# A deeper software pipeline in the second attention of a two-block transformer kernel: all-row score passes, later transposes and value products, an earlier start of the output projection

## The chip, the cores and the metric

The kernel runs on one core of a Trainium2 chip. The metric is the device time of one execution in microseconds (us). Engines are named as in the profile: PE is TensorE's matmul side, PEld its weight loads, DVE VectorE, ACT ScalarE, POOL GpSimd, SP SyncE, which issues the DMAs.

## The reference, cut to what matters

Two transformer blocks are computed for 512 tokens of width 1024. The part that the change concerns is the last mixer of the second block, a sliding-window attention with 16 query heads of 64, which share 4 key and value heads (so 4 heads make a group g), and its output projection:

```python
q, z = split(h @ w_in); q = q * 64 ** -0.5
# 4 blocks of 128 queries; each sees its own 128 keys and the 128 before
logits = q @ k.T + alibi; logits = where(valid, logits, -inf)
m = maximum(max(logits), sink)
p = exp(logits - m); denom = sum(p) + exp(sink - m)
out = (p @ v) / denom
y = (out * silu(z)) @ w_out
h = h + rms_norm(y, b_post_g)
```

All matrices are float32. The kernel reaches that precision with pairs of rounded numbers: an operand is split into a high part and a rest, and a product is made of three passes (high by high, high by rest, rest by high).

## The kernel before, in words

**Order by hand.** `tensor_order()` writes TensorE's whole work as one list of blocks, ORDER, and BLOCK gives each its number. TensorE walks the list; before a block it waits until the PSUM bank of the block has been emptied (`BEFORE`, `emptied`) and until its inputs are there (`ready`). The other engines walk loops of their own and wait for block numbers (`pe_block`) and for semaphores of one another. All queues are in order.

**Weights.** SP loads each unit of weights in two halves into a ring of four buffers, `raw`. POOL splits a half in `split_half`: for the input projection (`q5`, `z5`) it first multiplies the rows with the norm's gain (L567), then it waits until the unit that last used the slot of `whi` and `wlo` has been multiplied (`last_block`), and makes the high part (L580) and the rest (L587). There are two slots, so a unit can be split while its neighbour is in use.

**The second attention.** It has 16 steps, a group g and a query block b each (`STEPS2`, b running fastest). Steps with b = 0 see 128 keys, the others 256, so they have one or two key tiles kt. They are pipelined over slots (`SLOTS2`). In slot i TensorE does, in this order:

- `o5` of step i - 2: the value product, three passes of 512 columns for each key tile, into bank 3,
- `t5` of step i - 1: four transposes of probabilities for each key tile, into bank 6 or 7,
- `s5` of step i: the scores. For each of the four heads a pass with the high part of the keys (L1644) and one with their rest (L1645), into banks 4 and 5,
- one or two half blocks ("Fk" and "F", 12 passes of 512 columns each) of the input projection for later groups (`PARTS2`; one in slots 4, 8 and 12). Finished blocks go to banks 0, 1 and 2 in turn.

The queries of a head lie in `q5` on 128 rows: 64 hold the high part and 64 the rest. The keys' high part lies twice, on rows 0 to 63 and 64 to 127, and so does the rest. L1644 therefore runs on all 128 rows; L1645 uses the 64 rows of the queries' high part alone.

**The other engines in slot i.** DVE: `scores2(i)` (bias of the group when b = 0, L1351; four additions of bias with maximum, L1360; L1364 and L1366), the rests of the transposed probabilities of step i - 1 (L1407), `probs2(i)` (L1372, L1374 and four multiplications, L1378), then the emptying of finished input-projection blocks (L1396 for `q5`, L1415 for the gate `z5`) and the products with the gate (`MEET2`, L1426, L1419). ACT: copies of finished blocks, the high parts of the transposes (L930), the copies of the value product (L935), the exponentials of step i (L944, L945), and L948. Probabilities lie in `tok`, two buffers.

**Output projection.** Block ("T", "f", c, kh, t) adds, for tokens t and output half c, the products with features 512 kh to 512 kh + 511, 12 passes. Its bank is t + 4c. Units come in the order (c, kh) = (0,0), (0,1), (1,0), (1,1). Blocks (0, 0, t) for t = 1, 2 stand at the end of slot 15 and t = 0 in slot 17; the other 13 follow the slots. The last steps are squares on ACT (L650), the root on POOL, two products on DVE for each half and token (L1432, L1443), and the store.

Of the kernel before, what the change touches and what calls it, by code (L numbers as in the profile page):

```python
# [7 lines left out]
P = 128  # L8
S = 512
T = S // P  # L10
D = 1024
KD = D // P
HALF = 512
# [5 lines left out]
NQ, NKV, DH = 16, 4, 64  # L19
# [10 lines left out]
def weight_units():  # L30
# [25 lines left out]
    u += [("f", 2 * c + kh, "T", "b_w_out_2", 4 * kh, 512 * c) for c in range(2) for kh in range(2)]  # L56
# [23 lines left out]
SLOTS2 = 18  # L80
# [3 lines left out]
MEET2 = {f: max(4 * (f // 2) + 6 + f % 2 * (f < 6), 2 + min(i for i in DONE2 if ("z5", f) in DONE2[i])) for f in range(8)}  # L84

# [8 lines left out]
def tensor_order():  # L94
# [45 lines left out]
    for i in range(SLOTS2):  # L140
        if i == 17:
            o += [("T", "f", 0, 0, 0)]
        if 2 <= i < 18:
            o += [("o5", i - 2)]
        if 1 <= i < 17:
            o += [("t5", i - 1, kt) for kt in ((0, 1) if STEPS2[i - 1][1] else (1,))]
        if i == 0:
            o += PARTS2[-1]
        if i < 16:
            o += [("s5", i, m) for m in range(2)]  # L150
        o += PARTS2.get(i, [])
        if i == 15:
            o += [("T", "f", 0, 0, t) for t in (1, 2)]
    o += [("T", "f", 0, 0, 3)] + [("T", "f", 0, 1, t) for t in range(T)]
    o += [("T", "f", 1, kh, t) for kh in range(2) for t in range(T)]
# [7 lines left out]
def bank_of(b):  # L163

    kind = b[0]
    if kind == "tr":
        name, t, j = b[1:]
        return {"x": (2 * t + j) % 4, "p": 4 + j, "x1": t + 4 * j, "h": (2 * t + j) % 4,
                "n": (2 * t + j) % 4}[name]
    if kind in ("F", "Fa", "Fk"):  # L170
        s, f = b[1:]
        if s in ("z4", "u4"):
            return 4 * (f // 2 % 2) + f % 2 + 2 * (s == "u4")
        if s == "k5":
            return 6 + f
        if s in ("q5", "z5"):
            return ([("q5", 0), ("q5", 1)] + JOBS2).index((s, f)) % 3
        return [x[1:] for x in ORDER if x[0] == "F"].index((s, f)) % 4
    if kind in ("T", "Th"):
        s, c, _, t = b[1:]  # L180
        return t + 4 * (1 if s == "v" else (c + (s == "v4")) % 2)
# [35 lines left out]
def program(nc, x, p, pre_norm_gain, w_in, lambda_q1, lambda_k1, lambda_q2, lambda_k2, subln_gain,  # L217
# [9 lines left out]
    with ctx:  # L227
# [40 lines left out]
        mhalf = sb("mhalf", [P, 1])  # L268
        ss_attn, ms_attn, r_attn = (sb(n, [P, NH1, T]) for n in ("ss_attn", "ms_attn", "r_attn"))
# [43 lines left out]
        prob2 = lambda s: tok[:, s % 2, :].rearrange("p (h k) -> p h k", h=4)  # L313
# [109 lines left out]
        def last_block(n):  # L423
# [8 lines left out]
            return BLOCK["T", s, j // 2, j % 2, T - 1]  # L432
# [206 lines left out]
        def _(act):  # L639
# [279 lines left out]
            for i in range(SLOTS2 + 2):  # L919
# [7 lines left out]
                for kt in ((0, 1) if STEPS2[i - 1][1] else (1,)) if 1 <= i < 17 else ():  # L927
                    b = ("t5", i - 1, kt)
                    act.wait_ge(pe_block, BLOCK[b])
                    A(pThi(kt), psum[bank_of(b)][:, :], ACT.Copy).then_inc(pt_hi[kt], 1)  # L930
                if 2 <= i < 18:
                    g, b = STEPS2[i - 2]
                    act.wait_ge(pe_block, BLOCK["o5", i - 2])
                    for m in range(2):
                        A(o5[m * DH:(m + 1) * DH, 2 * g:2 * g + 2, b * P:(b + 1) * P],  # L935
                          psum[3][0:DH, :].rearrange("p (f m s) -> p m f s", f=2, m=2)[:, m], ACT.Copy)\
                            .then_inc(o5_copied, 1)
# [11 lines left out]
            for c in range(2):  # L949
                for t in range(T):  # L950
                    act.wait_ge(pe_block, BLOCK["T", "f", c, 1, t])
                    square("f", t, c, psum[t + 4 * c][:, :])
# [3 lines left out]
        def _(dve):  # L956
# [388 lines left out]
            def scores2(i):  # L1345
# [8 lines left out]
                if i >= 2:  # L1354
                    dve.wait_ge(pe_block, BLOCK["t5", i - 2, 1])
# [46 lines left out]
            for i in range(SLOTS2 + 2):  # L1402
                if i < 16:
                    scores2(i)
                for kt in ((0, 1) if STEPS2[i - 1][1] else (1,)) if 1 <= i < 17 else ():
# [24 lines left out]
            def f_gain(c, t):  # L1430
                dve.wait_ge(squared["f"], T * c + t + 1)
                V.tensor_tensor(part_(t, c), psum[t + 4 * c][:, :], gain[:, 1, c * HALF:(c + 1) * HALF], ALU.mult)\  # L1432
# [15 lines left out]
        def _(pe):  # L1448
# [120 lines left out]
            def work(b):  # L1569
# [65 lines left out]
                if kind == "s5":  # L1635
# [4 lines left out]
                    rows = slice(m * DH, (m + 1) * DH)  # L1640
                    for j in range(2):
# [3 lines left out]
                        ins = M(out_, q[rows], klo(g)[rows, keys], start=False, stop=True)  # L1645
# [46 lines left out]
```

## Time and profile before

| | before |
|---|---|
| median of 3 runs | 993.23 us (992.97 to 993.75) |
| profiled execution, span from first to last instruction | 992.1 us |
| around the span (median less span) | 1.1 us |
| mean granted TensorE clock over the span | 0.982 |
| PE busy in the span | 940.2 us |
| DVE, ACT, POOL busy in the span | 450.7, 267.9, 638.9 us |
| first scores of the second attention start | 774.3 us |
| last matmul of the kernel starts | 986.04 us |

The profiled execution's own time stands as its span plus what lies around it; it is taken that the 1.1 us around it are the same for every version. The second attention and its output projection are the last 218 us of the span. A row of the timeline gives start, duration, engine, line, operation, operands and, in brackets, the idle time of the engine before it with what ended it. Durations of matmuls overlap, since they are pipelined: what a matmul costs is the distance between two starts.

### The profile page before, as it was taken

To read this page: it belongs to the slowest core of one execution; us is meant where nothing else is said; L and a number is where in the kernel's file an instruction comes from. 1 tells how busy PE (TensorE), PEld (TensorE's weight loads), DVE (VectorE), ACT (ScalarE), POOL (GpSimd) and SP (SyncE) were. 2 spreads that over 40 slices of the span, in tenths; PEclk is the share of its full clock that TensorE was granted. 3 is DMA by queue.
4 is the path that set the end of the run, shared out by engine and by line. 5 is a ranking of instruction groups with operands and counts; after the bars stand their busy time and mean duration, and the time that the engine had idled before them with its cause. 6 is when DMAs were issued, how large, how long until landed. Compare 5 with 4: busy or idle time off the path is not lost.

```text
span 992.1 us, 11937 instructions
## 1 busy us (share of the span) xinstructions
PE 940.2 (95%) x4304; PEld 758.5 (76%) x4304; DVE 450.7 (45%) x821; ACT 267.9 (27%) x679; POOL 638.9 (64%) x702
## 2 busy tenths in 40 slices
PE   4999999899999989999999999999979999898997
PEld 3787778678887768888888888888768777666776
DVE  4123445655144370004545204444678566857543
ACT  4123323321133241114111111110134335434421
POOL 7676455547789576768777766777776665633333
PEclk9999999999999999999999999999999899988999
DMA  7343121232422313232322233222311211102102
GB/s 204 121 126 96 56 85 42 70 123 86 142 74 91 100 64 128 90 101 85 106 86 86 94 99 100 91 86 85 107 64 64 65 53 54 57 29 64 42 3 85
DMA packets 71865, 84.30 MB, mean 85 GB/s; under 512 B 11264, under 2 KB 53760, under 8 KB 71808
## 3 DMA queue, kind: packets, MB, share of 16 engines
q1 hardware_dynamic: 71808, 83.54, 26.5%
q8 instruction: 35, 0.57, 0.2%
q14 instruction: 22, 0.18, 0.1%
HBM read 81.44 MB, written 2.10 MB: 84 GB/s over the span
## 4 chain that ended last, share of the span: by engine, by line
PE 78%; DVE 9%; POOL 5%; ACT 4%; issue 2%; DMA 1%; SPq 0%; POOLq 0%; DVEq 0%; ACTq 0%
PE bank L1454 23%; PE bank L1455 23%; PE bank L1456 23%; DVE tok L1378 2%; POOL wlo L587 2%; PE bank L1645 2%; ACT tok L944 2%; PE bank L1644 2%; PE bank L1621 1%; PE bank L1650 1%; PE bank L1585 1%; POOL ms L539 1%; POOL rstd L542 1%; ACT junk L650 1%; PE bank L1584 1%
## 5 line engine op out<-in xcount | busy, mean ns | idle before, releaser
L580 POOL TENSOR_SCALAR whi<-raw 128x512 fp32r<-128x512 f32 x280 | 185.8, 681 | 309.9 <-PE bank L1456 304.8
L587 POOL TENSOR_TENSOR wlo<-raw,whi 128x512 fp32r<-128x512 f32 x280 | 382.8, 1388 | 0.0
L1454 PE MATMUL bank<-actB_hi,whi 128*128 128x512 f32 (+1 forms) x416 | 163.2, 392 | 0.8 <-POOL wlo L587 0.8
L1455 PE MATMUL bank<-actB_lo,whi 128*128 128x512 f32 (+1 forms) x416 | 160.4, 385 | 0.0
L1456 PE MATMUL bank<-actB_hi,wlo 128*128 128x512 f32 (+1 forms) x416 | 160.3, 385 | 0.0
L1454 PE MATMUL bank<-whi,actA_hi 128*128 128x512 f32 x304 | 122.3, 402 | 9.9 <-DVE actA_lo L970 6.4
L1456 PE MATMUL bank<-whi,actA_lo 128*128 128x512 f32 x304 | 120.3, 396 | 0.0
L1455 PE MATMUL bank<-wlo,actA_hi 128*128 128x512 f32 x304 | 120.2, 395 | 0.0
L1454 PEld LDWEIGHTS bank<-actB_hi,whi 128*128 128x128 f32 x416 | 79.5, 191 | 17.8 <-DVE big L1265 0.9
L1456 PEld LDWEIGHTS bank<-actB_hi,wlo 128*128 128x128 f32 x416 | 79.2, 190 | 15.7
L1455 PEld LDWEIGHTS bank<-actB_lo,whi 128*128 128x128 f32 x416 | 79.6, 191 | 14.6
L1454 PE MATMUL bank<-actA_hi,whi 128*128 128x512 f32 x224 | 90.0, 402 | 0.0
L1455 PE MATMUL bank<-actA_lo,whi 128*128 128x512 f32 x224 | 87.9, 393 | 0.0
L1456 PE MATMUL bank<-actA_hi,wlo 128*128 128x512 f32 x224 | 87.7, 392 | 0.0
L1454 PEld LDWEIGHTS bank<-whi,actA_hi 128*128 128x128 f32 x304 | 57.7, 190 | 24.6 <-DVE actA_lo L970 7.8
L1454 PE MATMUL bank<-whi,actB_hi 128*128 128x512 f32 x192 | 75.1, 391 | 0.0
L1456 PE MATMUL bank<-whi,actB_lo 128*128 128x512 f32 x192 | 74.7, 389 | 0.0
L1455 PE MATMUL bank<-wlo,actB_hi 128*128 128x512 f32 x192 | 74.7, 389 | 0.0
L1456 PEld LDWEIGHTS bank<-whi,actA_lo 128*128 128x128 f32 x304 | 58.2, 191 | 12.4
L1455 PEld LDWEIGHTS bank<-wlo,actA_hi 128*128 128x128 f32 x304 | 58.1, 191 | 11.7 <-issue 0.2
L1454 PEld LDWEIGHTS bank<-actA_hi,whi 128*128 128x128 f32 x224 | 42.4, 189 | 10.8 <-issue 1.7
L1456 PEld LDWEIGHTS bank<-actA_hi,wlo 128*128 128x128 f32 x224 | 42.5, 190 | 9.0
(196 smaller groups left out, 1347.5 us busy)
## 6 DMA issues: line engine op xcount, KB each, us to landing
raw<-in_a_w_in SPq DMA_DIRECT2D x48, 512.0 KB, 3.6
raw<-in_w_in SPq DMA_DIRECT2D x32, 512.0 KB, 3.7
raw<-in_a_w_out SPq DMA_DIRECT2D x16, 512.0 KB, 3.3
raw<-in_b_w_in SPq DMA_DIRECT2D x16, 512.0 KB, 3.3
raw<-in_w_out SPq DMA_DIRECT2D x8, 512.0 KB, 3.8
raw<-in_w_ple_gate SPq DMA_DIRECT2D x8, 512.0 KB, 3.2
raw<-in_b_w_out SPq DMA_DIRECT2D x8, 512.0 KB, 3.4
resid<-in_x SPq DMA_DIRECT2D x4, 512.0 KB, 7.8
```

Source lines behind the costliest of these rows:

```text
L539: pool.tensor_scalar(m, ss[:, n, t, 0:1], ss[:, n, t, 1:2], EPS, ALU.add, ALU.add).then_inc(ms_ready[name], 1)
L542: pool.tensor_tensor(rstd[:, n, t:t + 1], m, mhalf[:, 0:1], ALU.pow).then_inc(rstd_ready[name], 1)
L580: pool.tensor_scalar(H, src[:, i * HALF:(i + 1) * HALF], 1.0, 1.0, ALU.mult, ALU.mult).then_inc(w_hi, 1)
L587: ins = pool.tensor_tensor(L, src[:, i * HALF:(i + 1) * HALF], H.bitcast(f32), ALU.subtract)
L650: A(junk[:, :], src, ACT.Square, scale=1.0 / 32, accum_out=ss[:, NORMS[name], t, c:c + 1])\
L944: A(pr, pr, ACT.Exp, bias=nmx[:, h:h + 1], accum_out=rs[:, h:h + 1]).then_inc(exp5, 1)
L1378: V.tensor_scalar(pr, pr, rr[:, h:h + 1], None, ALU.mult).then_inc(prob5, 1)
L1454: M(out_, whi_, xhi_, start=start, stop=False)
L1455: M(out_, whi_, xlo_, start=False, stop=False)
L1456: return M(out_, wlo_, xhi_, start=False, stop=stop)
L1644: M(out_, q, khi(g)[:, keys], start=True, stop=False)
L1645: ins = M(out_, q[rows], klo(g)[rows, keys], start=False, stop=True)
```

## The change

The value product moves from two slots behind the scores to three, the transposes from one to two. On DVE the loop body now does the probabilities of step i - 1 first, then the rests of step i - 2's transposes, then the scores of step i; ACT has the value copies and the transposes first, then finished blocks, then the exponentials. A third probability buffer, `prob3`, is added; to make room the reserve for dynamic DMA descriptors is set to 1024. The second score pass uses all 128 rows, so that the product of the two rests is added as well. Units of the output projection come in the order (0,0), (1,0), (0,1), (1,1), and all eight blocks with kh = 0 run in slots 15 to 18, in other banks.

```diff
-    u += [("f", 2 * c + kh, "T", "b_w_out_2", 4 * kh, 512 * c) for c in range(2) for kh in range(2)]
+    u += [("f", 2 * c + kh, "T", "b_w_out_2", 4 * kh, 512 * c) for kh in range(2) for c in range(2)]
...
-SLOTS2 = 18
+SLOTS2 = 19
...
-MEET2 = {f: max(4 * (f // 2) + 6 + f % 2 * (f < 6), 2 + min(i for i in DONE2 if ("z5", f) in DONE2[i])) for f in range(8)}
+MEET2 = {f: max(4 * (f // 2) + (7 + f % 2 if f < 6 else 6), 2 + min(i for i in DONE2 if ("z5", f) in DONE2[i])) for f in range(8)}
+FIRST_F = {15: ((0, 0), (0, 1)), 16: ((0, 2), (0, 3)), 17: ((1, 0),), 18: ((1, 2), (1, 3), (1, 1))}
+BANKS_F = ((0, 1, 2, 4), (5, 3, 6, 7))
...
     for i in range(SLOTS2):
-        if i == 17:
-            o += [("T", "f", 0, 0, 0)]
-        if 2 <= i < 18:
-            o += [("o5", i - 2)]
-        if 1 <= i < 17:
-            o += [("t5", i - 1, kt) for kt in ((0, 1) if STEPS2[i - 1][1] else (1,))]
+        if 3 <= i:
+            o += [("o5", i - 3)]
+        if 2 <= i < 18:
+            o += [("t5", i - 2, kt) for kt in ((0, 1) if STEPS2[i - 2][1] else (1,))]
...
-        if i == 15:
-            o += [("T", "f", 0, 0, t) for t in (1, 2)]
-    o += [("T", "f", 0, 0, 3)] + [("T", "f", 0, 1, t) for t in range(T)]
-    o += [("T", "f", 1, kh, t) for kh in range(2) for t in range(T)]
+        o += [("T", "f", c, 0, t) for c, t in FIRST_F.get(i, ())]
+    o += [("T", "f", c, 1, t) for c in range(2) for t in range(T)]
...
-        prob2 = lambda s: tok[:, s % 2, :].rearrange("p (h k) -> p h k", h=4)
+        prob2 = lambda s: (tok[:, 0, :], tok[:, 1, :], prob3[:, :])[s % 3].rearrange("p (h k) -> p h k", h=4)
...
-            for i in range(SLOTS2 + 2):
+            for i in range(SLOTS2 + 1):
+                if 1 <= i < 17:
+                    probs2(i - 1)
+                for kt in ((0, 1) if STEPS2[i - 2][1] else (1,)) if 2 <= i < 18 else ():
+                    dve.wait_ge(pt_hi[kt], i - 1 if kt else kt0_steps(i - 2))
+                    V.tensor_tensor(pTlo(kt), psum[bank_of(("t5", i - 2, kt))][:, :], pThi(kt).bitcast(f32),
+                                    ALU.subtract).then_inc(pt_lo[kt], 1)
                 if i < 16:
                     scores2(i)
-                for kt in ((0, 1) if STEPS2[i - 1][1] else (1,)) if 1 <= i < 17 else ():
-                    dve.wait_ge(pt_hi[kt], i if kt else kt0_steps(i - 1))
-                    V.tensor_tensor(pTlo(kt), psum[bank_of(("t5", i - 1, kt))][:, :], pThi(kt).bitcast(f32),
-                                    ALU.subtract).then_inc(pt_lo[kt], 1)
-                if i < 16:
-                    probs2(i)
...
                         M(out_, q, khi(g)[:, keys], start=True, stop=False)
-                        ins = M(out_, q[rows], klo(g)[rows, keys], start=False, stop=True)
+                        ins = M(out_, q, klo(g)[:, keys], start=False, stop=True)
...
-    nc = bacc.Bacc("TRN2", target_bir_lowering=False, num_devices=1)
+    nc = bacc.Bacc("TRN2", target_bir_lowering=False, num_devices=1, dynamic_dma_scratch_size=1024)
```

## Rows read from the trace of the kernel before

**Rows 1.** Waits of PE, 770 us to the end: waiter, releaser, us, times, longest.

```profile
PE bank L1650 <- DVE tok L1378: 10.2, 8, 3.6
```

**Rows 2.** PE's timeline in slots 1 and 2 of the attention.

```profile
783.76 0.63 PE L1650 MATMUL bank<-ident,tok 128*128 128x128 f32 x4 [1.80 <-DVE tok L1378]
...
785.06 0.55 PE L1645 MATMUL bank<-rests,parts 64*128 64x256 f32 x1
...
791.59 0.57 PE L1454 MATMUL bank<-actB_hi,whi 128*128 128x512 f32 x1
...
795.90 1.03 PE L1650 MATMUL bank<-ident,tok 128*128 128x128 f32 x8
796.69 0.36 PE L1644 MATMUL bank<-parts 128*128 128x256 f32 x1
...
799.17 0.50 PE L1454 MATMUL bank<-actB_hi,whi 128*128 128x512 f32 x1
```

**Rows 3.** The rest-of-keys pass, line 1645: ns min/median/max, first and last start.

```profile
L1645 PE MATMUL bank<-rests,parts x64: 322/381/580, 774.5 to 936.2; 64*128 64x256 f32 x48, 64*128 64x128 f32 x16
```

**Rows 4.** PE's timeline in the value projection: 256 columns, all rows, 21 steps between.

```profile
736.45 0.28 PE L1456 MATMUL bank<-v5hi,actB_lo 128*128 128x256 f32 x1
...
738.94 0.28 PE L1456 MATMUL bank<-v5hi,actB_lo 128*128 128x256 f32 x1
```

**Rows 5.** PE's timeline in the last 12 output blocks, 143 steps between.

```profile
953.53 0.47 PE L1454 MATMUL bank<-whi,actA_hi 128*128 128x512 f32 x1
...
986.04 0.39 PE L1456 MATMUL bank<-whi,actA_lo 128*128 128x512 f32 x1
```

**Rows 6.** Windows of 5 us: length, busy by engine, granted clock, DMA.

```profile
785.00:790.00 5.00, 5.00 (x12) 3.33 (x12) 2.73 (x11) 0.99 (x5) 0.00 (x0) 0.51 0.01 3
```

**Rows 7.** DVE's timeline: scores in slot 11, bias and scores in slot 12.

```profile
891.93 0.48 DVE L1360 CUSTOM_DVE_ANT_0 tok<-bank,smA,sinks 128x256 f32<-128x256 f32 x1
...
893.90 1.01 DVE L1364 TENSOR_SCALAR nmx<-mx 128x4 f32<-128x4 f32 x1
...
901.90 0.90 DVE L1351 TENSOR_SCALAR smB<-smC 128x256 f32<-128x256 f32 x4
...
904.03 0.17 DVE L1364 TENSOR_SCALAR nmx<-mx 128x4 f32<-128x4 f32 x1
```

**Rows 8.** DVE's timeline in slot 14, from the maxima to the probabilities.

```profile
927.33 0.17 DVE L1364 TENSOR_SCALAR nmx<-mx 128x4 f32<-128x4 f32 x1
...
927.61 1.28 DVE L1407 TENSOR_TENSOR pT<-bank,pT 128x512 fp32r<-128x512 f32 x2
929.93 0.16 DVE L1372 TENSOR_TENSOR den<-rs,esk 128x4 f32<-128x4 f32 x1 [1.04 <-ACT esk L945]
...
930.35 1.14 DVE L1378 TENSOR_SCALAR tok<-tok,rr 128x256 f32<-128x256 f32 x4
```

**Rows 9.** DVE's timeline in slot 3: the same four multiplications.

```profile
813.50 3.57 DVE L1378 TENSOR_SCALAR tok<-tok,rr 128x256 f32<-128x256 f32 x4
```

**Rows 10.** POOL's timeline: rests made in slot 3, and one unit split in slots 6 and 7.

```profile
813.80 2.63 POOL L587 TENSOR_TENSOR wlo<-raw,whi 128x512 fp32r<-128x512 f32 x2
...
834.45 1.20 POOL L580 TENSOR_SCALAR whi<-raw 128x512 fp32r<-128x512 f32 x2 [10.24 <-PE bank L1456]
...
841.21 2.55 POOL L587 TENSOR_TENSOR wlo<-raw,whi 128x512 fp32r<-128x512 f32 x2
```

**Rows 11.** Groups of instructions by form, 790 us to the end (busy us, mean ns).

```profile
L1378 DVE TENSOR_SCALAR tok<-tok,rr 128x256 f32<-128x256 f32 x48 | 20.0, 480 | 0.4
...
L1378 DVE TENSOR_SCALAR tok<-tok,rr 128x128 f32<-128x128 f32 x12 | 7.6, 698 | 0.1
...
L1366 DVE TENSOR_TENSOR den<-sinks,nmx 128x4 f32<-128x4 f32 x14 | 5.9, 421 | 0.5
L1364 DVE TENSOR_SCALAR nmx<-mx 128x4 f32<-128x4 f32 x14 | 5.7, 410 | 0.5
```

**Rows 12.** DVE's timeline: the last gate block, z5 of feature tile 7, emptied.

```profile
943.62 0.68 DVE L1415 SCALAR_TENSOR_TENSOR zg<-th,bank 128x512 f32<-128x512 f32 x1
```

More of the change, by code:

```diff
@@ L180, in bank_of @@
         s, c, _, t = b[1:]
+        if s == "f":
+            return BANKS_F[c][t]
         return t + 4 * (1 if s == "v" else (c + (s == "v4")) % 2)
@@ L268, in program @@
         mhalf = sb("mhalf", [P, 1])
+        prob3 = sb("prob3", [P, D])
         ss_attn, ms_attn, r_attn = (sb(n, [P, NH1, T]) for n in ("ss_attn", "ms_attn", "r_attn"))
@@ L431, in last_block @@
                 return BLOCK["F", s, 2 * j + 1]
-            return BLOCK["T", s, j // 2, j % 2, T - 1]
+            return max(BLOCK["T", s, j // 2, j % 2, t] for t in range(T))
         block = ctx.enter_context(nc.Block())
@@ L918, in _ @@
                 q5_out(f)
-            for i in range(SLOTS2 + 2):
+            for i in range(SLOTS2 + 1):
+                if 3 <= i < 19:
+                    g, b = STEPS2[i - 3]
+                    act.wait_ge(pe_block, BLOCK["o5", i - 3])
+                    for m in range(2):
+                        A(o5[m * DH:(m + 1) * DH, 2 * g:2 * g + 2, b * P:(b + 1) * P],
+                          psum[3][0:DH, :].rearrange("p (f m s) -> p m f s", f=2, m=2)[:, m], ACT.Copy)\
+                            .then_inc(o5_copied, 1)
+                for kt in ((0, 1) if STEPS2[i - 2][1] else (1,)) if 2 <= i < 18 else ():
+                    b = ("t5", i - 2, kt)
+                    act.wait_ge(pe_block, BLOCK[b])
+                    A(pThi(kt), psum[bank_of(b)][:, :], ACT.Copy).then_inc(pt_hi[kt], 1)
                 for s, f in DONE2.get(i - 1, ()):
@@ L926, in _ @@
                         A(th[:, :], psum[bank_of(("F", s, f))][:, :], ACT.Tanh, scale=0.5).then_inc(z5_tanh, 1)
-                for kt in ((0, 1) if STEPS2[i - 1][1] else (1,)) if 1 <= i < 17 else ():
-                    b = ("t5", i - 1, kt)
-                    act.wait_ge(pe_block, BLOCK[b])
-                    A(pThi(kt), psum[bank_of(b)][:, :], ACT.Copy).then_inc(pt_hi[kt], 1)
-                if 2 <= i < 18:
[L932 to L937, printed above, removed]
                 if i < 16:
@@ L950, in _ @@
                 for t in range(T):
-                    act.wait_ge(pe_block, BLOCK["T", "f", c, 1, t])
-                    square("f", t, c, psum[t + 4 * c][:, :])
+                    b = ("T", "f", c, 1, t)
+                    act.wait_ge(pe_block, BLOCK[b])
+                    square("f", t, c, psum[bank_of(b)][:, :])
         @block.vector
@@ L1353, in scores2 @@
                     dve.wait_ge(bias2_made, 4 * g + 4)
-                if i >= 2:
-                    dve.wait_ge(pe_block, BLOCK["t5", i - 2, 1])
+                if i >= 3:
+                    dve.wait_ge(pe_block, BLOCK["t5", i - 3, 1])
                 for h in (0, 2, 1, 3):
@@ L1401, in _ @@
             dve.wait_ge(dist_made, 4)
-            for i in range(SLOTS2 + 2):
+            for i in range(SLOTS2 + 1):
+                if 1 <= i < 17:
+                    probs2(i - 1)
+                for kt in ((0, 1) if STEPS2[i - 2][1] else (1,)) if 2 <= i < 18 else ():
+                    dve.wait_ge(pt_hi[kt], i - 1 if kt else kt0_steps(i - 2))
+                    V.tensor_tensor(pTlo(kt), psum[bank_of(("t5", i - 2, kt))][:, :], pThi(kt).bitcast(f32),
+                                    ALU.subtract).then_inc(pt_lo[kt], 1)
                 if i < 16:
                     scores2(i)
-                for kt in ((0, 1) if STEPS2[i - 1][1] else (1,)) if 1 <= i < 17 else ():
-                    dve.wait_ge(pt_hi[kt], i if kt else kt0_steps(i - 1))
-                    V.tensor_tensor(pTlo(kt), psum[bank_of(("t5", i - 1, kt))][:, :], pThi(kt).bitcast(f32),
-                                    ALU.subtract).then_inc(pt_lo[kt], 1)
-                if i < 16:
-                    probs2(i)
                 for f in (f for s, f in DONE2.get(i - 1, ()) if s == "q5"):
@@ L1431, in f_gain @@
                 dve.wait_ge(squared["f"], T * c + t + 1)
-                V.tensor_tensor(part_(t, c), psum[t + 4 * c][:, :], gain[:, 1, c * HALF:(c + 1) * HALF], ALU.mult)\
+                V.tensor_tensor(part_(t, c), psum[bank_of(("T", "f", c, 1, t))][:, :],
+                                gain[:, 1, c * HALF:(c + 1) * HALF], ALU.mult)\
                     .then_inc(f_gained, 1)
@@ L1639, in work @@
                     keys = slice((blk - 1) * P + k0, (blk + 1) * P)
-                    rows = slice(m * DH, (m + 1) * DH)
                     for j in range(2):
```

## The prediction

> **What bounds the kernel now.** I read the waits of PE first, then its timeline, then the queues that it waits for. PE is nearly always at work, but three things make the second attention long. The first is waits: eight times PE stood before a transpose until DVE had multiplied the probabilities, 10.2 us in all [rows 1]. The second is the clock. After the 1.80 us gap the matmuls of slot 1 soon stand twice as far apart, from about 785.1 to 791.9 us [rows 2], and the granted clock in that window is 0.51, the lower of the two levels, 1.2 GHz [rows 6]. Half of these 6.8 us is lost, 3.4 us. In the timeline the same follows the two other gaps of over 1.5 us in this stage, so 10.2 us in all. The third is the score passes themselves: in slot 2 eight of them take 799.17 - 796.69 = 2.48 us, 0.31 us each, though they have only 256 columns [rows 2]. Elsewhere passes of 256 columns on all 128 rows, each with a new weight load, start every 2.49 / 21 = 0.119 us [rows 4]. In the scores 128-row and 64-row passes alternate. The row speaks for that alternation as the price, not the columns. From the first to the last score pass of the stage there are 161.7 us [rows 3], about 10.7 us a slot.
>
> **All-row passes.** No row shows this alternation on all rows; the nearest is the value projection [rows 4], the same in columns, rows and alternating loads. I take 0.119 us, so 16 x 8 x 0.119 = 15.2 us instead of 16 x 8 x 0.31 = 39.7 us. Bounds: 0.31 (nothing won) and 0.10, what a transpose of 128 columns costs (0.79 us for eight, [rows 2]). The added arithmetic, rest by rest, has no instruction of its own.
>
> A page speaks against this part: the Trainium skill, "TensorE: Matmul & The Clock Gate", Part 3, says that a weight load overlaps a running matmul only where their row groups differ. By that rule two all-row passes overlap no better than before and the term stays 39.7 us; by the row it is 15.2 us. The value projection has equal row groups throughout and does not bear the rule out [rows 4].
>
> **PE's sum, if it never waited.** A 512-column pass costs 32.51 / 143 = 0.2273 us [rows 5], so a half block or an output block of 12 passes 2.73 us and a key tile of the value product 0.68 us. Four transposes cost 0.40 us [rows 2]. From the first score (774.3 us) to the end of the last score block (slot 15) PE now does 27 half blocks, 73.7 us; all scores, 15.2; value products of steps 0 to 12, 22 key tiles, 15.0; transposes of steps 0 to 13, 24 key tiles, 9.5. That is 113.4 us, up to 887.7 us. After it come 16 output blocks, 43.7 us, three value products, 4.1, and two steps of transposes, 1.6: 49.4 us.
>
> **The new loop over DVE and ACT.** With the deeper pipeline, probabilities are needed two slots later, so the old wait [rows 1] goes. What is late next is the loop that no depth shortens: DVE scores step i, ACT takes the exponentials, DVE multiplies, makes the rests of the transposes and only then scores step i + 1. From rows: scores to maxima 893.90 - 891.93 = 1.97 us [rows 7]; maxima to the first probability instruction, with the exponentials between, 929.93 - 927.33 = 2.60 us; two small instructions 0.42 us, four multiplications 1.14 us, two rests 1.28 us [rows 8]. Together 7.41 us. Bias and scores of a b = 0 step take 2.13 us in place of 1.97 [rows 7], and one slot in four has only one rest (0.64 us less), so 7.3 us on average. Other DVE work of a slot (emptied blocks, gate products) fits under the exponentials.
>
> To this comes what POOL does to DVE. The four multiplications took 1.14 us in slot 14 but 3.57 us in slot 3 [rows 8, 9], where POOL made two rests for 2.63 us [rows 10]. Against 0.285 us for a multiplication and 0.17 us for a small instruction [rows 8], the groups hold 20.0 - 13.7, 7.6 - 3.4, 5.7 - 2.4 and 5.9 - 2.4 us too much [rows 11], 17.3 us in some 15 slots, 1.2 a slot. No row shows how these meetings fall in the new order. Bounds: 0, and 1.9 if shorter slots bring more of them. I take 0.8, two thirds of the measured mean, because PE's full slots (two half blocks, scores, two key tiles: about 8.6 us) hide part of a stall. So 8.1 us a slot.
>
> On this the Trainium skill, "SBUF — State Buffer", section "SBUF: two separate sides", says that the port pair shared by the two engines is held for one whole instruction, so the loser would wait for one. By that, a stall would be half of what these rows suggest, the loop 7.7 us a slot, and the time that of rival (a). The trace shows a stall of 2.43 us, longer than either of the two POOL instructions [rows 9, 10].
>
> **Where PE and DVE meet.** In the new list the first output block (c = 0, t = 0) has bank 0, and the last block in it is z5 of tile 7, finished at the end of slot 14. DVE empties it (L1415) only after scores2(15). In the kernel before this gate came at 943.62 us [rows 12], and blocks t = 1 and 2, in other banks, stood in its place. So PE stops after the last scores for DVE's scores (1.97 + 0.29), the gate (0.6) and handovers (0.2), 3.1 us and the rests before them, and whatever DVE lags behind is paid here. A gap of 1.80 us was followed by the low clock [rows 2]; I add one such fall, 3.4 us (bounds 0 and 6.8).
>
> DVE's scores of step 2 start at the earliest when PE reaches them: 774.3 + three score blocks (2.9) + four half blocks (10.9) + one tile of transposes (0.4) = 788.5 us. With 13 slots of 8.1 us scores2(15) starts at 893.8, PE goes on at 896.9. Adding 49.4 and 3.4 gives 949.7 us for the last matmul; from there to the end of the span it was 992.1 - 986.4 = 5.7 us and nothing there changes. Span 955.4 us, and with the 1.1 us around it 956.5 us.
>
> **Edits that cost nothing.** Output weights: a slot is free after slot 16 and again after slot 18. Splitting an unscaled unit takes the 9.3 us of a scaled one [rows 10] less 1.84 us of scaling, 7.5 us; slots 17 and 18 give the first 14 us of cover, and the four blocks (0,1,t) give the second 10.9 us. Without that cover each would cost its 7.5 us. SP issues the same loads, in the changed order, and POOL the same splits. The last value copy and gate products come at the end of slot 18 under three output blocks, 8.2 us. The third buffer takes no instruction. The smaller descriptor reserve concerns no queue that the page lists for data; I price it at 0, with no row against it.
>
> **The rivals.** (a) PE bounds the stage: the meetings with POOL hide in PE's full slots. Then scores2(15) starts 0.6 us after the last scores, at 888.3, PE goes on at 891.4 and the time is 951.0 us with the fall of the clock, 947.6 without it. For it: PE's 113.4 us over 16 slots are 7.1 us a slot and full slots are longer than the bare loop. Against it: slots 4, 8 and 12 have one half block and the loop has no slack there. (b) POOL's stalls keep their mean or grow. At 1.2 us a slot scores2(15) starts at 899.0 and the time is 961.7 us; at 1.9, 970.8. For it: POOL's work is squeezed into less time. Against it: much of it may fall where DVE waits for PE. (c) All-row passes win nothing. PE's sum is 24.5 us more, DVE's loop hides, and the time is 975.5 us. Against it: rows 4. (d) Slower: each slot makes PE wait at its head for DVE (bank 4 scored, rests made), and each wait brings the clock down. A fall costs 3.4 us and at least the 1.8 us before it [rows 2], 5.2 us. From 947.6 us it takes more than nine falls to pass 993.2; ten give 999.6 us. For it: a gap of that size did this three times. Against it: a slot at half clock makes PE late, so that the next one has no gap, and two half blocks (5.5 us) stand between a slot's scores and the next slot's head.
>
> **How the numbers follow.** I give the forecast 0.55, (a) 0.22, (b) 0.16, (c) 0.04 and (d) 0.03. The range runs from 946, below (a) without a fall, to 971, the upper end of (b); (c) and (d) lie outside it, and some of the rest. About 0.2% (2 us) is what a measurement here can tell from no change. Slower comes from (d), 0.03; the same only from a mixture of (c) and (d), 0.01; the rest is faster.
>
> **What would show it.** Right: eight score passes in about 0.95 us; no wait of a transpose for L1378; one PE gap of 3 us or more before the first output block, ended by L1415, and a granted clock near 0.5 behind it; about 120 us from the first to the last score pass. Wrong: score passes still 0.31 us apart; gaps in front of every slot with low clock; waits of PE for POOL's L587 in the output projection; or no gap before the first output block.

## The result and the profile after

| | before | after |
|---|---|---|
| median | 993.49 us (four runs, 992.97 to 996.85) | 971.51 us (four runs, 967.63 to 974.51) |
| ratio | 1 | 0.9753, 95% interval 0.9722 to 0.9783 |
| profiled execution | span 992.1 us | 969.13 us, span 967.4 us |
| first maxima (L1364, after L1368) to the end of the span | 214.2 us | 190.6 us |
| us a slot, slots 2 to 15, by those maxima | 10.57 | 8.85 |

The kernel is faster by 22.0 us by the medians and by 24.7 us by the spans of the profiled executions; 36.7 us were forecast. The median lies 0.5 us above the upper end of the range, 971; the ratio times the 993.23 us that the forecast started from gives 968.7 us, which lies inside. Two measures are used below, "stage" (the row "first maxima to the end") and "us a slot", because they leave out what varies ahead of the stage: the first maxima come anywhere from 776.7 to 784.0 us in the ten profiled executions of the variants, which differ little there in code.

The page of the kernel after, engines and clock:

```profile
PE 909.9 (94%) x4304; PEld 747.7 (77%) x4304; DVE 456.6 (47%) x821; ACT 268.8 (28%) x679; POOL 638.1 (66%) x702
...
PEclk9999999999999999999999999999999999999899
```

PE has 30 us less busy time than the 940.2 us before. Most of it is the score passes: with them alone put back (E1) the page has 935.9 us.

PE's timeline of the kernel after (start, us, engine, line, operands; idle time before and what ended it in brackets): the eight score passes of slot 1, the two longest gaps, the last matmul.

```profile
779.53 0.28 PE L1648 MATMUL bank<-parts 128*128 128x256 f32 x1
...
780.48 0.40 PE L1459 MATMUL bank<-actB_hi,whi 128*128 128x512 f32 x1
...
810.50 0.42 PE L1459 MATMUL bank<-pT,parts 128*64 128x512 f32 x1 [3.64 <-DVE pT L1411]
...
904.00 0.28 PE L1649 MATMUL bank<-rests,parts 128*128 128x256 f32 x1
...
910.31 0.80 PE L1459 MATMUL bank<-whi,actA_hi 128*128 128x512 f32 x1 [6.04 <-DVE zg L1419]
...
913.47 0.50 PE L1460 MATMUL bank<-wlo,actA_hi 128*128 128x512 f32 x1
...
961.34 0.39 PE L1461 MATMUL bank<-whi,actA_lo 128*128 128x512 f32 x1
```

Eight passes now take 780.48 - 779.53 = 0.95 us, 0.119 us each, against 2.48 us in [rows 2] (1.03 us in the slots where they follow transposes). The wait of transposes for the multiplications [rows 1] has no row left. In its place stand these, from the waits of PE, 770 us to the end (waiter, releaser, us, times, longest):

```profile
PE bank L1459 <- DVE pT L1411: 8.3, 5, 3.6
...
PE bank L1459 <- DVE zg L1419: 6.0, 1, 6.0
...
PE bank L1648 <- DVE mx L1364: 2.1, 2, 1.4
```

The value product now waits for the rests that DVE makes of the transposed probabilities (L1411), and once PE waits 6.0 us for the gate (L1419). Who sets the pace is clearer from DVE's side. Groups of DVE in the stage of the kernel after, 776 to 915 us (busy us, mean ns; idle time before them):

```profile
L1382 DVE TENSOR_SCALAR tok<-tok,rr 128x256 f32<-128x256 f32 x32 | 16.9, 589 | 0.3
L1411 DVE TENSOR_TENSOR pT<-bank,pT 128x512 fp32r<-128x512 f32 x24 | 15.6, 683 | 2.2 <-ACT pT L933 2.0
L1382 DVE TENSOR_SCALAR prob<-prob,rr 128x256 f32<-128x256 f32 x16 | 9.5, 657 | 0.1
...
L1370 DVE TENSOR_TENSOR den<-sinks,nmx 128x4 f32<-128x4 f32 x16 | 7.0, 436 | 0.5
L1364 DVE CUSTOM_DVE_ANT_0 tok<-bank,smA,sinks 128x256 f32<-128x256 f32 x16 | 6.8, 478 | 0.0
...
L1376 DVE TENSOR_TENSOR den<-rs,esk 128x4 f32<-128x4 f32 x16 | 6.2, 387 | 15.2 <-ACT esk L948 15.1
...
L1368 DVE TENSOR_SCALAR nmx<-mx 128x4 f32<-128x4 f32 x16 | 4.8, 298 | 0.6
...
L1355 DVE TENSOR_SCALAR smB<-smC 128x256 f32<-128x256 f32 x8 | 3.7, 520 | 0.0
L1355 DVE TENSOR_SCALAR smA<-smC 128x256 f32<-128x256 f32 x4 | 3.4, 918 | 0.0
L1382 DVE TENSOR_SCALAR tok<-tok,rr 128x128 f32<-128x128 f32 x12 | 3.4, 348 | 0.1
...
L1382 DVE TENSOR_SCALAR prob<-prob,rr 128x128 f32<-128x128 f32 x4 | 0.9, 283 | 0.0
```

The scores (L1364) never stood idle for PE (0.0), and the rests waited for PE's transposes, through ACT's copies, for 2.0 us in the whole stage. Nearly all the rest of DVE's idle time is the exponentials inside the loop (L1376 for ACT, 15.1 us). So DVE and ACT set the pace and PE waits for them. The same groups in the kernel before, 777 to 942 us, three of them:

```profile
L1360 DVE CUSTOM_DVE_ANT_0 tok<-bank,smA,sinks 128x256 f32<-128x256 f32 x24 | 10.7, 482 | 16.0 <-PE bank L1645 15.8
...
L1372 DVE TENSOR_TENSOR den<-rs,esk 128x4 f32<-128x4 f32 x15 | 4.3, 288 | 18.3 <-ACT esk L945 18.3
...
L1351 DVE TENSOR_SCALAR smB<-smC 128x256 f32<-128x256 f32 x8 | 2.1, 326 | 0.0
```

There the scores still waited for PE: 16.0 us in this group alone.

The chain of waits of the kernel after, slots 13 to 15 (start, us, what), shows the loop without a stall and with one:

```profile
893.12 0.18 DVE nmx L1368
...
896.14 0.92 DVE tok L1382 x4
...
897.19 0.68 DVE pT L1411
...
899.53 0.18 DVE nmx L1368
...
902.80 1.65 DVE prob L1382 x2
...
904.49 1.97 DVE prob L1382 x2
906.46 1.19 DVE pT L1411 x2
...
909.29 0.18 DVE nmx L1368
...
909.58 0.69 DVE zg L1419
...
910.31 0.80 PE bank L1459
```

No piece of PE lies between 893.12 and 910.31. Slot 13 to 14 takes 6.41 us; slot 14 to 15 takes 9.76 us, because the four multiplications begin at 902.80 and end at 906.46, 3.66 us in place of 1.14. POOL's timeline in the same kernel:

```profile
903.09 2.60 POOL L590 TENSOR_TENSOR wlo<-raw,whi 128x512 fp32r<-128x512 f32 x2
```

Two rests by POOL, from 903.09 to 905.69, cover the stall. One by one, the multiplications take 0.48, 1.37, 1.35 and 0.70 us: the second and the third each end with one of the two rests, the last with the high part (L583) that POOL makes next. So an instruction of DVE loses to one instruction of POOL at a time. It is so all over the stage: of the kinds L1355, L1368, L1370, L1376 and L1382, 38 instructions take over 0.15 us more than their bare time, all 38 end at most 0.2 us behind the end of an instruction of POOL, and none loses more than that instruction took. This is the pair [rows 9, 10] again, now on the path that sets the end.

### The profile page after: what moved, and what is told of

It reads as the page before. It is cut to its first block, busy times and chain, and to the rows that moved or that the text cites. A ratio compares the mean times of both kernels' runs of the same rounds, so it can differ in the third digit from the quotient of the medians.

```text
span 967.4 us, 11936 instructions
## 1 busy us (share of the span) xinstructions
PE 909.9 (94%) x4304; PEld 747.7 (77%) x4304; DVE 456.6 (47%) x821; ACT 268.8 (28%) x679; POOL 638.1 (66%) x702
## 4 chain that ended last, share of the span: by engine, by line
PE 72%; DVE 14%; POOL 5%; ACT 5%; issue 3%; DMA 1%; SPq 0%; POOLq 0%; DVEq 0%; ACTq 0%
PE bank L1459 22%; PE bank L1460 22%; PE bank L1461 22%; POOL wlo L590 2%; ACT tok L947 2%; DVE tok L1382 2%; DVE tok L1364 2%; DVE pT L1411 1%; PE bank L1626 1%; PE bank L1590 1%; POOL ms L542 1%; POOL rstd L545 1%; ACT junk L653 1%; PE bank L1589 1%; PE bank L1599 1%
## 5 line engine op out<-in xcount | busy, mean ns | idle before, releaser
L583 POOL TENSOR_SCALAR whi<-raw 128x512 fp32r<-128x512 f32 x280 | 184.8, 678 | 286.1 <-PE bank L1461 280.8
L1459 PE MATMUL bank<-actB_hi,whi 128*128 128x512 f32 (+1 forms) x416 | 159.8, 384 | 0.8 <-POOL wlo L590 0.8
L1461 PEld LDWEIGHTS bank<-actB_hi,wlo 128*128 128x128 f32 x416 | 78.4, 188 | 15.1
L1460 PEld LDWEIGHTS bank<-actB_lo,whi 128*128 128x128 f32 x416 | 78.4, 189 | 14.2
L1459 PEld LDWEIGHTS bank<-actA_hi,whi 128*128 128x128 f32 x224 | 42.0, 188 | 10.7 <-issue 1.7
```

Source lines behind the costliest of these rows:

```text
L583: pool.tensor_scalar(H, src[:, i * HALF:(i + 1) * HALF], 1.0, 1.0, ALU.mult, ALU.mult).then_inc(w_hi, 1)
L1459: M(out_, whi_, xhi_, start=start, stop=False)
L1460: M(out_, whi_, xlo_, start=False, stop=False)
L1461: return M(out_, wlo_, xhi_, start=False, stop=stop)
```

## The experiments

The theory after the result: DVE's loop sets the pace, lengthened by POOL's stalls, and the gap before the first output block comes on top. The rival is that PE sets the pace. E1 and E2 split the change in its two halves, E3 takes out the gap, E4 to E7 take stalls or work out of the loop, E8 changes the form of the multiplications, E9 doubles POOL's subtractions and E10 moves the bias. Each is an edit of the kernel after, except E2.

| | ratio to before, interval | stage, us | us a slot | DVE waits for the transposes, to 915 us |
|---|---|---|---|---|
| after | 0.9753 (0.9722 to 0.9783) | 190.6 | 8.85 | 2.0 us |
| E1 half rows | 0.9841 (0.9797 to 0.9885) | 196.8 | 9.18 | 7.1 |
| E2 old order, all rows | 0.9850 (0.9815 to 0.9885) | 197.9 | 9.68 | none (scores wait for PE 12.5) |
| E3 bank order | 0.9649 (0.9608 to 0.9690) | 180.7 | 8.9 | 2.0 |
| E4 no POOL rests | 0.9670 (0.9632 to 0.9708) | 179.2 | 8.22 | 11.4 |
| E5 no scaling | 0.9695 (0.9655 to 0.9736) | 184.5 | 8.47 | 2.0 |
| E6 multiplications on ACT | 0.9596 (0.9553 to 0.9639) | 170.5 | 8.16 | 23.3 |
| E7 neither | 0.9657 (0.9613 to 0.9701) | 180.3 | 8.22 | 16.5 |
| E8 form with sum output | 0.9603 (0.9560 to 0.9646) | 175.5 | 8.49 | 4.9 |
| E9 rests made twice | 0.9901 (0.9871 to 0.9930) | 201.3 | 9.54 | 2.0 |
| E10 bias early | 0.9517 (0.9477 to 0.9558) | 166.3 | 7.84 | 18.2 |

E6, E8 and E10 hold the edit of E3 as well. In E1 and E9 the last scores come only after 915 us, so their last column misses the end of the stage.

**E1.** The second score pass goes back to 64 rows.

```diff
-    ins = M(out_, q, klo(g)[:, keys], start=False, stop=True)
+    ins = M(out_, q[m * DH:(m + 1) * DH], klo(g)[m * DH:(m + 1) * DH, keys], start=False, stop=True)
```

> The changed kernel with the second score pass back on 64 rows; everything else stays. Theory (the loop over DVE and ACT, lengthened by POOL's stalls, paces the stage at the measured 8.85 us a slot): PE's work grows by 24.5 us to about 138 us, 8.6 us a slot, which still fits under the loop most of the time, so the time goes up by 2 to 10 us only, to 971 to 979 us. Rival (PE paces the stage and the all-row passes are what was won): the time goes up by the whole 24 us, to about 993 us.

Measured: median 978.64 us. The source view of the second pass in E1 (ns minimum, median, maximum; first and last start) and PE's only long gap:

```profile
L1649 PE MATMUL bank<-rests,parts x64: 322/380/384, 779.2 to 916.7; 64*128 64x256 f32 x48, 64*128 64x128 f32 x16
```

```profile
921.37 0.80 PE L1459 MATMUL bank<-whi,actA_hi 128*128 128x512 f32 x1 [4.25 <-DVE zg L1419]
```

By the distances of the starts PE has about 22 us more work (a score block 2.48 us in place of 1.03, one of 128 columns 2.01 in place of 0.92); the 24.5 us expected counted all 16 blocks at 256 columns. The stage is 6.2 us longer. The waits for L1411 are gone: PE took the time that it had spent waiting. In the slots of E1 PE has no gap, so there PE sets the pace, 9.18 us, a little above that of the loop. So in the kernel after some seven tenths of what the all-row passes save on PE is returned as waiting and as the low clock behind it.

**E2.** The kernel before, with the all-row passes alone.

```diff
-    ins = M(out_, q[rows], klo(g)[rows, keys], start=False, stop=True)
+    ins = M(out_, q, klo(g)[:, keys], start=False, stop=True)
```

> The kernel before with all-row score passes and nothing else. Theory (loop): in the old order transposes, scores, exponentials and probabilities stand in one chain, 0.8 + 0.95 + 2.3 + 2.6 + 1.6 us and POOL's stalls of 1.3 us, about 9.6 us a slot in place of 10.7, and the low clock after PE's waits stays; the time comes to 974 to 984 us, so the deeper pipeline has a share of its own. Rival (PE paces, depth is worth nothing): 24 us less, about 969 us, the time of the changed kernel.

Measured: median 979.5 us. The waits of PE in E2:

```profile
PE bank L1650 <- DVE tok L1378: 16.3, 8, 3.7
```

The old wait [rows 1] grew from 10.2 to 16.3 us. By the ratios, times 993.2 us: the passes alone win 14.9 us, the pipeline alone (E1) 15.8, both 24.5. The parts overlap by 6.2 us, and by the stages by 17.4 + 16.3 - 23.6 = 10.1 us. The intervals reach some 3 to 4 us to each side, so by the ratios alone the overlap is not clear of noise; the stages, which leave out what varies ahead of them, show it. Each part alone meets another bound: E1 that of PE, E2 the chain in which scores wait for PE (12.5 us) and transposes for DVE (16.3 us), and both together the loop over DVE and ACT. "The pipeline" holds the earlier output blocks too; no run takes them apart.

**E3.** The last gate block holds bank 0, and the first output block wanted it. Two blocks with other banks go first.

```diff
-FIRST_F = {15: ((0, 0), (0, 1)), 16: ((0, 2), (0, 3)), 17: ((1, 0),), 18: ((1, 2), (1, 3), (1, 1))}
+FIRST_F = {15: ((0, 1), (0, 2)), 16: ((0, 0), (0, 3)), 17: ((1, 0),), 18: ((1, 2), (1, 3), (1, 1))}
```

> The changed kernel with token tiles 1 and 2 of the output projection in slot 15 and tiles 0 and 3 in slot 16, so that bank 0, which the last gate block holds, is wanted two blocks later. Theory: the gap of 6.0 us before the first output block goes, and with it the 3.2 us at half clock behind it (1.6 us); 961 to 964 us against 969 in a like run. Rival (what DVE lags behind is paid at the next wait, transposes of step 15 or the value product of step 14): the time stays within 2 us.

Measured: median 959.0 us. The waits of PE in E3, 770 us to the end:

```profile
PE bank L1459 <- DVE pT L1411: 8.2, 5, 3.0
PE bank L1648 <- DVE mx L1364: 2.0, 2, 1.3
PE bank L1648 <- issue: 0.8, 1, 0.8
```

The 6.0 us for L1419 are gone and nothing took their place. By the ratios E3 is 10.3 us below after, by the stage 9.9. From the maxima of slot 15 to the end it takes 50.1 us in place of 58.1, 8.0 us less: in the main the gap of 6.0 and the low clock behind it (1.6). The pace in the slots is untouched (8.9). In the kernel before the same stretch took 54.5 us: as built, the changed end of the stage was 3.6 us slower than the old one, and only this order makes it faster.

**E4.** POOL leaves out the subtractions for the input projection's units.

```diff
+    no_rest = sb("no_rest", [P, 1])
...
+    if s in ("q5", "z5") and not by_dve:
+        pool.wait_ge(w_hi, 2 * n + 2)
+        pool.memset(no_rest[:, :], 0.0).then_inc(w_lo, 1)
+        return
```

> The changed kernel without POOL's subtractions for the input-projection units from z5 0 on (their rests of the weights stay what the buffer held, so the output is not the reference's); POOL's scaling and high parts stay. Theory (POOL's subtractions stall DVE's multiplications and small instructions by about 1.5 us a slot): the four multiplications take 1.14 us nearly everywhere, a slot takes 7.3 to 8 us, and the time is 950 to 958 us. Rival (the loop is slow for another reason, such as ACT's order or handovers): multiplications of 3.4 us remain, or the slot stays at 8.8 us, and the time is within 3 us of the changed kernel.

Measured: median 961.96 us, 8.22 us a slot, a stage 11.4 us shorter. PE's gap before the first output block in E4:

```profile
903.35 0.80 PE L1464 MATMUL bank<-whi,actA_hi 128*128 128x512 f32 x1 [7.84 <-DVE zg L1424]
```

The direction is right and the size smaller than expected (950 to 958 us): from slot 2 to 11 PE has no gap and sets the pace, 70.9 / 9 = 7.88 us, so that DVE waits for it (11.4 us); from 11 to 15 a slot takes 9.0 us, since the output units' rests are still made; and 1.8 us were given back in the longer gap.

**E5.** POOL scales one column instead of a unit's rows.

```diff
-    for k in range(4):
-        pool.tensor_scalar(src[:, k * 256:(k + 1) * 256], src[:, k * 256:(k + 1) * 256],
-                           bg[:, 4 * (n % 2) + k:4 * (n % 2) + k + 1], 1.0, ALU.mult,
-                           ALU.mult).then_inc(w_scaled, 1)
-    scaled[0] += 4
+    pool.tensor_scalar(src[:, 0:1], src[:, 0:1], bg[:, 4 * (n % 2):4 * (n % 2) + 1], 1.0, ALU.mult,
+                       ALU.mult).then_inc(w_scaled, 1)
+    scaled[0] += 1
```

> The changed kernel with POOL's row scaling of the input-projection units left out but for one column (the gain is missing from those weights, so the output is not the reference's); the subtractions stay. It separates the two kinds of POOL work: without the subtractions a slot still took 8.2 us and several multiplications 2.0 us. Theory (scaling stalls DVE as well, about 0.5 us a slot): 8.2 to 8.5 us a slot and 5 to 9 us less from the first maxima to the end than the changed kernel's 190.6 us. Rival (only the subtractions stall DVE): 8.8 us a slot, within 2 us.

Measured: median 962.77 us, 8.47 us a slot, a stage 6.1 us shorter. The scaling stalls DVE too. The timelines of DVE and POOL in the kernel after have such a stall by itself, 0.41 us in place of 0.16 while POOL only scales:

```profile
794.47 0.41 DVE L1370 TENSOR_TENSOR den<-sinks,nmx 128x4 f32<-128x4 f32 x1
793.01 1.85 POOL L570 TENSOR_SCALAR raw<-raw,bg 128x256 f32<-128x256 f32 x4
```

The 6.1 us are half of E4's 11.4, but those were capped by PE's pace, so the scaling's share is at most that. Without it POOL's other work also comes at other times; how much of the 6.1 us is that, no run separates.

**E6.** The four multiplications move from DVE to ACT, behind ACT's copies of the transposes.

```diff
+    if 1 <= i < 17:
+        act.wait_ge(rec5, i)
+        for h in range(4):
+            pr = prob2(i - 1)[:, h, (0 if STEPS2[i - 1][1] else P):256]
+            A(pr, pr, ACT.Copy, scale=rr[:, h:h + 1]).then_inc(prob5, 1)
...
-    for h in range(4):
-        pr = prob2(i)[:, h, k0:256]
-        V.tensor_scalar(pr, pr, rr[:, h:h + 1], None, ALU.mult).then_inc(prob5, 1)
```

> The changed kernel with the output blocks in the order of the third experiment, and with the four multiplications of a step by one over the denominator moved from DVE to ACT (4 x 0.5 us behind the copies of the transposes); the same values are computed. Theory (DVE's loop and its meetings with POOL pace the stage): the loop loses 1.14 us and its most stalled instruction, ACT's queue becomes the pace at 7.2 to 7.8 us a slot, and the time is 944 to 952 us. Rival (ACT has no room: exponentials wait for the multiplications in its queue and the loop is as long as before): 8.5 us a slot or more, 956 us or more.

Measured: median 952.77 us, 8.16 us a slot: 0.8 us above the expected range, and the pace lies between the two theories. DVE waits 23.3 us for transposes and PE only 3.2 us in the whole stage, so PE paces most slots. PE's two longer waits, 1.03 and 2.02 us for the rests (L1413), stand in slots 10 and 14, two slots behind a new bias: there the stalled bias still sets the pace.

**E7.** The edits of E4 and E5 together.

> The changed kernel without POOL's subtractions and without its scaling for the input-projection units from z5 0 on (both missing from the weights, so the output is not the reference's); only the high parts are made. Theory: with POOL quiet the bare loop or PE's own sum shows, 7.2 to 7.6 us a slot, multiplications of 1.14 us, and 172 to 176 us from the first maxima to the end. Rival (something else lengthens the loop): 8.2 us a slot as without the subtractions alone.

Measured: median 959.51 us, 8.22 us a slot, the rival's number. But the mean hides two stretches. From slot 2 to 11 it is 70.1 / 9 = 7.79 us, PE without a gap; from slot 11 to 15 it is 9.2 us, where POOL makes the output units' rests, which this edit keeps (multiplications of 3.11 and 3.60 us there). A quiet POOL gives PE's pace; the edit was not as quiet as meant.

**E8.** The multiplications stay on DVE, in the form that also writes a sum.

```diff
+    psums = sb("psums", [P, 4])
...
-    V.tensor_scalar(pr, pr, rr[:, h:h + 1], None, ALU.mult).then_inc(prob5, 1)
+    V.tensor_scalar(pr, pr, rr[:, h:h + 1], 0.0, ALU.mult, ALU.add,
+                    accum_out=psums[:, h:h + 1]).then_inc(prob5, 1)
```

> The kernel of the third experiment (output blocks reordered) with the four multiplications left on DVE but in the form that also writes out a sum, which is not used; the same probabilities. Theory (DVE's multiplication is stalled because of the form in which it runs, not because it is on DVE while POOL works): each group of four takes the same time in every slot, somewhat longer than the free 1.14 us, 1.5 to 1.9 us, with no group of 2 us or more; the slots from 2 to 15 take 8.3 to 8.8 us instead of 8.9. Rival (any DVE instruction between SBUF and SBUF waits for POOL's subtractions): groups of 3.3 us and more remain and a slot takes 9.2 us or more.

Measured: median 956.22 us, 8.49 us a slot (E3: 959.0, 8.9). Groups of DVE in the stage of E8:

```profile
L1383 DVE TENSOR_SCALAR_CACHE_REDUCE tok<-tok,rr 128x256 f32<-128x256 f32 x32 | 13.4, 477 | 0.3
L1371 DVE TENSOR_TENSOR den<-sinks,nmx 128x4 f32<-128x4 f32 x16 | 8.5, 533 | 0.5
```

This form costs 0.40 us from start to start, more than the 0.285 us of [rows 8], and it is never stalled: every group of four over 256 columns takes 1.68 us, also beside POOL's rests. The small instruction L1371 still is, at 0.53 us on average for 4 columns. The Trainium skill, "SBUF — State Buffer", section "Who interferes with whom", says that the form of tensor_scalar that writes out its accumulator does not take the port pair shared with POOL; the trace agrees, 1.68 us in every slot with 256 columns against 1.14 to 3.66 us of the plain form.

**E9.** Each of POOL's subtractions is made once more, into a spare buffer.

```diff
+    spare = sb("spare", [P, HALF])
...
+    if s in ("q5", "z5") and not by_dve:
+        pool.tensor_tensor(spare[:, :], src[:, i * HALF:(i + 1) * HALF], H.bitcast(f32),
+                           ALU.subtract).then_inc(spared, 1)
...
```

> The changed kernel with each of POOL's subtractions for the input-projection units made once more, into a spare buffer. Theory (POOL's subtractions stall DVE in the loop): more and longer stalls, multiplications of 4 us and more, 9.3 to 10 us a slot, 6 to 15 us more than the changed kernel; PE does not wait for POOL, whose unit then takes 14.4 us and must be ready within two slots, about 17 us. Rival (the stalls are a matter of when a unit is released, and the loop has slack to take them in): within 3 us of the changed kernel.

Measured: median 985.73 us, by the ratios (0.9901 - 0.9753) x 993.2 = 14.7 us above after, 9.54 us a slot. The waits of PE in E9:

```profile
PE bank L1468 <- DVE pT L1420: 13.4, 7, 4.5
PE bank L1468 <- DVE zg L1428: 7.9, 1, 7.9
PE bank L1468 <- POOL wlo L597: 3.2, 2, 2.3
```

POOL's added 30 us (668.1 us busy against 638.1) make PE's waits for L1420, the rests, grow from 8.3 to 13.4 us and the gap from 6.0 to 7.9. Against the expectation PE also waited twice for POOL, 3.2 us, so of the 10.7 us that the stage grew not all is stalls; and of the groups of four multiplications only one passed 4 us (4.22).

**E10.** E6, and the bias of the next group is made two slots early, while ACT takes exponentials, instead of ahead of the scores that need it.

```diff
...
+    if i == 0:
+        dve.wait_ge(pe_block, BLOCK["v5", T - 1])
+        make_bias(0)
...
+    if i < 12 and i % 4 == 2:
+        make_bias(i // 4 + 1)
```

> The kernel with multiplications on ACT and reordered output blocks, in which DVE also makes the bias of the next group two slots earlier, behind the scores of the third step of a group, where it waits for exponentials anyway. Theory (DVE's loop still paces the slots 4, 8 and 12, where the bias and its stalls stand in it): 3 to 6 us less than that kernel, 946 to 950 us, and no PE gap before the value product in slots 9 and 13. Rival (PE's sum or ACT's queue paces those slots): no change, 951 to 954 us.

Measured: median 947.15 us, 7.84 us a slot, the fastest of all, 4.8% below the kernel before. Its interval just touches that of E6. Groups of DVE in the stage of E10:

```profile
L1417 DVE TENSOR_TENSOR pT<-bank,pT 128x512 fp32r<-128x512 f32 x28 | 18.2, 687 | 18.3 <-ACT pT L933 18.2
...
L1356 DVE TENSOR_SCALAR smB<-smC 128x256 f32<-128x256 f32 x8 | 6.2, 831 | 0.0
```

DVE now waits 18.2 us for the transposes, and the view of PE's waits has no row at all in the stage: PE is the bound. The bias is still stalled (this group 0.83 us each on average, 0.52 in the kernel after), but it now lies beside the exponentials, and no wait of PE comes of it.

## Why the prediction was right or wrong

**Right: all-row passes.** 0.119 us was taken from [rows 4], and 0.95 to 1.04 us for eight of 256 columns is what they take. The rule of Part 3 of "TensorE: Matmul & The Clock Gate" in the Trainium skill, by which a weight load overlaps a running matmul only where the row groups differ, would by the prediction's working have left them at 0.31 us; the trace does not agree, and with it rival (c) falls.

**Right: what is late next.** The wait of [rows 1] is gone and the loop over DVE and ACT is the pace (the chain of waits, E1). The gap before the first output block is there, ended by the gate, with low clock behind it. From the first to the last score pass it takes 904.00 - 773.14 = 130.9 us, against 161.7 before and the 120 of the forecast: the order of what is late is right, the length of a slot is not.

**Wrong: the term c = 0.8 us a slot for POOL's stalls, "two thirds of the measured mean, because PE's full slots ... hide part of a stall".** The step had two faults. First, nothing hid. With the bare durations of the prediction, but for 128 columns, where its 0.285 us was too much, the four kinds that it counted hold too much by

- L1382, 256 columns: 16.9 + 9.5 - 48 x 0.285 = 12.7 us,
- L1382, 128 columns (0.22 us in the slots without a stall): 3.4 + 0.9 - 16 x 0.22 = 0.8 us,
- L1370 and L1368: 7.0 + 4.8 - 32 x 0.17 = 6.4 us.

That is 19.9 us over 16 slots, 1.24 a slot, the mean of before [rows 11]. POOL did the same work and took the same toll of these four, in slots a sixth shorter. PE's full slots could not hide any of it: a stall sits in the loop, and PE's cover counts only where the loop waits for PE, 2.0 us in all. Second, two kinds were not counted: L1376 holds 6.2 - 16 x 0.17 = 3.5 us too much and the bias (L1355) 3.7 + 3.4 - 12 x 0.225 = 4.4 us, 0.49 a slot; in the kernel before they held 4.3 - 15 x 0.17 = 1.8 us and, in the group shown, 2.1 - 8 x 0.225 = 0.3 us. So the whole toll grew: with the same bare times the groups of the kernel before, 777 to 942 us, hold about 21.5 us too much, those of the kernel after 27.8.

Together 1.73 us a slot. The bare loop was the other way off: 6.41 us with one rest, and 9.76 less 2.52 and 0.25 of stalls (L1382, L1376), 6.99 us, with two, where the prediction had 6.77 and 7.41; more than half of that is the 1.97 us from scores to maxima, 909.29 - 907.57 = 1.72 here. This error took back part of the other. By these rows a slot is 6.9 + 1.73, and 0.15 of waiting for transposes: 8.8, measured 8.85. In the prediction's terms c was 8.85 - 7.3 = 1.55, inside its bounds of 0 to 1.9.

The prediction also held that a stall of 2.43 us is longer than either of POOL's two instructions. That counts four multiplications as one: each instruction by itself lost no more than one of POOL's, as in slot 14 above. What made the toll high is that several instructions of a slot lose one after the other.

The same working, against the span of 955.4 us: the first score came 1.2 us early (773.1). Slots 0 and 1, for which no stall was counted, were full of them, and scores2(2) started 19.4 us behind the first score instead of 14.2: +5.2. DVE's timeline of the kernel after there, two of the stalls, and at the last scores:

```profile
784.82 1.22 DVE L1370 TENSOR_TENSOR den<-sinks,nmx 128x4 f32<-128x4 f32 x1
...
788.91 2.96 DVE L1382 TENSOR_SCALAR tok<-tok,rr 128x256 f32<-128x256 f32 x4
...
792.51 0.48 DVE L1364 CUSTOM_DVE_ANT_0 prob<-bank,smA,sinks 128x256 f32<-128x256 f32 x1
...
907.57 0.47 DVE L1364 CUSTOM_DVE_ANT_0 tok<-bank,smB,sinks 128x256 f32<-128x256 f32 x1
```

Thirteen slots of (907.57 - 792.51) / 13 = 8.85 us instead of 8.1: +9.8. From there to the output block 2.74 us instead of 3.1, -0.4; from the output block to the end of the last matmul, with a fall of the clock that cost 1.6 us (half of the 3.2 us to 913.47) instead of 3.4, -1.4. The tail is equal. The sum is +12.0, and the span 967.4.

**The rivals.** What came is (b), the stalls keep their mean or grow, to which 0.16 was given; its 961.7 to 970.8 us hold the profiled execution (969.1), and the median lies 0.7 us above. The reason given against it, that much may fall where DVE waits for PE, could have been tested by the rule that a loop which sets the pace has no such place. For (a), PE bounds, the condition is met in the changed kernel only where DVE waits its 2.0 us for transposes; it is met in the slots of E1, from slot 2 to 11 in E4 and E7, and throughout in E10. PE's pace there is 7.84 us a slot: the prediction divided 113.4 us by 16 slots, but slots 0 and 1 hold only 14.2 of them, and over the others it is 99.2 / 13 = 7.6. The clock did not fall in every slot (d): over slots 0 to 14, 776 to 905 us, the mean granted clock is 0.97. It fell behind single waits, as after the 3.64 us at 810.50 (0.66 in the 5 us from 810); this cost PE time while the loop set the pace.

The range missed the median by 0.5 us, less than the runs of one kernel differ (967.63 to 974.51). Its upper end was (b) with c at its bound; the 5.2 us of slots 0 and 1 stood in no bound of it.

## What to carry to other kernels

Once a loop over two engines sets the pace, nothing beside it hides its stalls: price it with every stall that its instructions show, small ones too, and take no share of it off as hidden: here POOL did the same work in a shorter stage, and the toll did not fall but grew (21.5 to 27.8 us). Read who waits for whom from both sides; a scores group with 0.0 us of idle time says more than PE's 94%. The way out is to move the stalled instructions to an engine without that conflict (E6), to a form without it (E8), or to a place where the loop waits anyway (E10), and to give the first block behind a loop a bank that does not hang on the loop's end (E3).

## What was not expected of the hardware

The stalls come one to one: the 2.52 us lost in slot 14 are three multiplications that each waited for one instruction of POOL, two rests and a high part. So the loss goes by how many instructions of DVE meet one of POOL's, and by how long POOL's takes, not by the size of DVE's: an instruction of DVE over only 4 columns, 0.17 us bare, took up to 1.30 us (L1376). POOL's scaling and high parts, one input and one output, stall DVE as its subtractions do, only less, as they are shorter: a multiplication beside a high part took 0.70 us. DVE's instructions that read a PSUM bank never lost anything in the stage: the scores (L1364) took 0.48 us at most and the rests (L1411) 0.69, whatever POOL did.

After the 6.04 us gap PE's passes stood at half clock for 3.2 us, after the 1.80 us gap of [rows 2] for 6.8 us. The windows of the kernel after (length, busy by engine, granted clock, DMA):

```profile
905.00:910.00 5.00, 0.00 (x0) 0.00 (x0) 4.93 (x15) 0.31 (x1) 4.38 (x5) 0.68 0.32 105
910.00:915.00 5.00, 4.69 (x14) 3.75 (x15) 2.34 (x8) 2.38 (x10) 0.00 (x0) 0.63 0.32 105
```

The granted clock is already down while PE does nothing (0.68), so this gap paid part of the low stretch itself. The length of a gap alone does not give it: behind the 3.64 us gap at 810.50 the 5 us from 810 have 0.66, about 3.4 us of low clock. Why the clock ahead of the stage differs between executions, and the first maxima with it by up to 7 us, stays open.
